# State space scan: which engine sums the four turning products, where they are kept, and how the cosine's argument is made

## The reference, cut to what matters

```
a_re, a_im = mag * cos(ang), mag * sin(ang)
bu = einsum('blgc,gpc->blgp', u, bb)            # complex input to each state
s[t] = a * s[t-1] + bu[t]                       # complex, over the 512 tokens
y = einsum('blgp,gcp->blgc', s_re, c_re) - einsum('blgp,gcp->blgc', s_im, c_im) + d * u
```

```
s_re = z0*cos - z1*sin
s_im = z0*sin + z1*cos
y    = C0 . s_re + C2 . s_im                     # C0, C2: scaled output matrices, summed over states
```

## Time and profile before

| | us |
|---|---|
| median of 3 runs (lowest to highest) | 3302.62 (3302.15 to 3303.47) |
| the profiled execution, whole / its span | 3305.22 / 3303.4 |
| PE busy | 2876.7 (87%) |
| DVE busy | 1712.5 (52%) |
| ACT busy | 1058.2 (32%) |
| POOL busy | 173.4 (5%) |

### The profile page before, as it was taken

How to read it: one execution, slowest core, us unless ns; L and a number is a source line. 1 busy time by engine, 2 the same in 40 slices (tenths; PEclk the granted TensorE clock), 3 DMA queues, 4 the chain that set the end, 5 groups by cost and what they waited for, 6 DMA issues and landing times.

```text
span 3303.4 us, 35265 instructions
## 1 busy us (share of the span) xinstructions
PE 2876.7 (87%) x13044; PEld 2335.9 (71%) x13044; DVE 1712.5 (52%) x2707; ACT 1058.2 (32%) x1557; POOL 173.4 (5%) x152
## 2 busy tenths in 40 slices
PE   2989996999999798889879998777667798999999
PEld 1865585999999477767658886545444577888887
DVE  8657776554645444334254443333688743444443
ACT  3334424221221423222342223343333232232222
POOL 0000000000000000000000000000666000000000
PEclk7989998999999878877989999876788897999999
DMA  5300051322323001000112222110111121222222
GB/s 202 111 32 1 1 171 53 128 96 99 126 98 122 24 13 39 32 20 26 59 56 95 95 95 83 51 39 26 45 48 48 48 87 45 96 95 95 94 90 95
DMA packets 68002, 237.97 MB, mean 72 GB/s; under 512 B 7680, under 2 KB 8192, under 8 KB 67776
## 3 DMA queue, kind: packets, MB, share of 16 engines
q1 hardware_dynamic: 64224, 229.23, 20.6%
q10 hardware_dynamic: 3680, 7.42, 0.7%
HBM read 234.52 MB, written 2.10 MB: 72 GB/s over the span
## 4 chain that ended last, share of the span: by engine, by line
PE 75%; DVE 17%; ACT 4%; issue 3%; DMA 0%; POOL 0%; ACTq 0%; DVEq 0%; SPq 0%
PE DP L416 20%; PE DP L418 19%; PE DP L417 19%; PE XP L787 2%; PE XP L1065 2%; DVE PR L2175 2%; PE XP L909 2%; DVE TQ L2171 2%; PE XP L529 1%; DVE MPROD L476 1%; DVE TQ L556 1%; DVE PR L2165 1%; DVE HL L545 1%; PE DP L929 1%; PE XP L999 1%
## 5 line engine op out<-in xcount | busy, mean ns | idle before, releaser
L416 PE MATMUL DP<-HH,WL 128*128 128x512 f32 (+1 forms) x1920 | 743.2, 387 | 118.0 <-DVE WL L409 72.2
L417 PE MATMUL DP<-HH,WH 128*128 128x512 f32 (+1 forms) x1920 | 716.4, 373 | 0.0
L418 PE MATMUL DP<-HL,WH 128*128 128x512 f32 (+1 forms) x1920 | 715.3, 373 | 0.0
L409 DVE TENSOR_TENSOR WL<-RAW,WH 128x1024 fp32r<-128x1024 f32 x327 | 400.5, 1225 | 338.8 <-ACT WH L400 328.7
L416 PEld LDWEIGHTS DP<-HH,WL 128*128 128x128 f32 x1920 | 371.3, 193 | 193.2 <-DVE WL L409 82.8
L416 PE MATMUL DP<-A,WL 128*128 128x384 f32 (+1 forms) x1296 | 476.5, 368 | 21.7 <-DVE A L2202 11.1
L400 ACT ACTIVATE WH<-RAW 128x1024 fp32r<-128x1024 f32 x327 | 343.7, 1052 | 467.2 <-PE DP L418 413.1
L418 PE MATMUL DP<-A,WH 128*128 128x384 f32 (+1 forms) x1296 | 471.7, 364 | 0.0
L417 PE MATMUL DP<-A,WH 128*128 128x384 f32 (+1 forms) x1296 | 471.6, 364 | 0.0
L417 PEld LDWEIGHTS DP<-HH,WH 128*128 128x128 f32 x1920 | 369.8, 193 | 57.4 <-issue 13.3
L418 PEld LDWEIGHTS DP<-HL,WH 128*128 128x128 f32 x1920 | 368.5, 192 | 47.3
(11 more groups left out here) (322 smaller groups left out, 3544.3 us busy)
## 6 DMA issues: line engine op xcount, KB each, us to landing
RAW<-in_stream SPq DMA_DIRECT2D x423, 512.0 KB, 3.3
MATS<-in_ssm ACTq DMA_DIRECT2D x16, 256.0 KB, 2.6
X<-in_x SPq DMA_DIRECT2D x8, 384.0 KB, 9.8
BW<-in_rel ACTq DMA_DIRECT2D x4, 512.0 KB, 3.6
out<-X SPq DMA_DIRECT2D x8, 256.0 KB, 2.4
COND<-in_cond SPq DMA_DIRECT2D x1, 1024.0 KB, 5.0
CONST<-in_const SPq DMA_DIRECT2D x1, 256.0 KB, 5.0
COS<-in_rope SPq DMA_DIRECT2D x1, 256.0 KB, 11.6
```

The source lines that it names most:

```text
L409: dve.tensor_tensor(WL[:, w, :], RAW[:, nxt.u % RING, :], WH[:, w, :].bitcast(F32), ALU.subtract).then_inc(raw_done[nxt.u % RING], 1)
L416: pe.matmul(out, al, bh, start=first, stop=False)
L417: pe.matmul(out, ah, bh, start=False, stop=False)
L418: return pe.matmul(out, ah, bl, start=False, stop=last)
```

## The change

Four things are done together.

- **The sums.** VectorE's two sums of products (L2178) go. TensorE multiplies all four products and adds them up in PSUM: CM(0) with the first, CM(3) with the second, CM(2) with the third and the fourth. CM(3), which was scratch, now holds minus CM(0), made by a new GpSimd instruction.
- **The tile.** The four products go to a tile of their own, PAIRS, in place of PR. It lies at the address of HH, whose columns for the context tokens aren't used in this stage.
- **The waits.** The wait for `ssm_out` on VectorE moves from ahead of the first products (L2165 before) to ahead of the last products. TensorE waits for each product by itself.
- **The cosine.** cos(x) is taken as sin(quarter turn - |x|). ScalarE makes the magnitude (`Abs`) from TURN into TR, and GpSimd's L685 and L687 go.

```diff
+        with ExitStack() as s7:
+            PAIRS = sb(s7, "PAIRS", [P, KT, T])
...
+        def TURNED(k):
+            return PAIRS[:, 2 * k:2 * k + 2, LAT:T]
...
             def turns(i):
                 pool.tensor_tensor(TURN[:, :], TURN[:, :], TR[:, 0:LAT], ALU.subtract).then_inc(sem("ssm_turns"), 1)
-                pool.wait_ge(sem("ssm_turns"), 2 * i + 1)
-                pool.tensor_scalar(TR[:, 0:LAT], TURN[:, :], 0.25, None, ALU.is_gt).then_inc(sem("turn_back"), 1)
-                pool.wait_ge(sem("turn_back"), i + 1)
-                pool.tensor_tensor(TR[:, 0:LAT], TURN[:, :], TR[:, 0:LAT], ALU.subtract).then_inc(sem("ssm_turns"), 1)
...
             def outputs_scaled(i):
                 pool.tensor_tensor(CM(2), CM(1), CM(2), ALU.subtract).then_inc(sem("ssm_c"), 1)
+                pool.wait_ge(sem("ssm_c"), 3 * i + 1)
+                pool.tensor_scalar(CM(3), CM(0), -1.0, None, ALU.mult).then_inc(sem("ssm_c"), 1)
...
             def ssm_outputs(i):
-                pe.wait_ge(sem("ssm_c"), 2 * i + 2)
+                pe.wait_ge(sem("ssm_c"), 3 * i + 3)
...
-                for q, k in enumerate((0, 2)):
-                    pe.wait_ge(sem("ssm_state"), 2 * i + q + 1)
-                    last = pe.matmul(XP[:, 2 + t % 2, :], CM(k), PR[:, k, :], start=(j == 0 and q == 0), stop=(j == 3 and q == 1))
+                for k, c in enumerate((0, 3, 2, 2)):
+                    pe.wait_ge(sem("ssm_products"), 4 * i + k + 1)
+                    last = pe.matmul(XP[:, 2 + t % 2, :].rearrange("p (a n) -> p a n", a=2), CM(c), TURNED(k),
+                                     start=(j == 0 and k == 0), stop=(j == 3 and k == 3))
...
             def trig(i):
-                act.wait_ge(sem("ssm_turns"), 2 * i + 1)
+                act.wait_ge(sem("ssm_turns"), i + 1)
+                act.activation(TR[:, 0:LAT], TURN[:, :], ACT.Abs).then_inc(sem("turn_back"), 1)
                 act.activation(TRIG[:, i % 2, 0, :], TURN[:, :], ACT.Sin, scale=TWO_PI).then_inc(sem("ssm_trig"), 1)
-                act.wait_ge(sem("ssm_turns"), 2 * i + 2)
-                act.activation(TRIG[:, i % 2, 1, :], TR[:, 0:LAT], ACT.Sin, scale=TWO_PI, bias=QUARTER[:, 0:1]
+                act.wait_ge(sem("turn_back"), i + 1)
+                act.activation(TRIG[:, i % 2, 1, :], TR[:, 0:LAT], ACT.Sin, scale=-TWO_PI, bias=QUARTER[:, 0:1]
                                ).then_inc(sem("ssm_trig"), 1)
...
             def turned(i):
                 if i:
                     dve.wait_ge(sem("ssm_products"), 4 * i)
-                    dve.wait_ge(sem("ssm_out"), i)
...
                 dve.wait_ge(sem("ssm_z"), 2 * i + 2)
+                if i:
+                    dve.wait_ge(sem("ssm_out"), i)
                 for k, (z, q) in enumerate([(0, cos), (1, sin), (0, sin), (1, cos)]):
-                    dve.tensor_tensor(PR[:, k, :], TQ[:, z, 0:LAT], q, ALU.mult).then_inc(sem("ssm_products"), 1)
-                dve.wait_ge(sem("ssm_products"), 4 * i + 4)
-                for z, op in ((0, ALU.subtract), (2, ALU.add)):
-                    dve.tensor_tensor(PR[:, z, :], PR[:, z, :], PR[:, z + 1, :], op).then_inc(sem("ssm_state"), 1)
+                    dve.tensor_tensor(TURNED(k), TQ[:, z, 0:LAT].rearrange("p (a n) -> p a n", a=2),
+                                      q.rearrange("p (a n) -> p a n", a=2), ALU.mult).then_inc(sem("ssm_products"), 1)
```

More of the change, by code:

```diff
@@ L1541, in _ @@
                     if i >= 1:
-                        act.wait_ge(sem("ssm_c"), 2 * i)
+                        act.wait_ge(sem("ssm_c"), 3 * i)
                         act.wait_ge(sem("ssm_driven"), i)
```

## The result

| | before | after |
|---|---|---|
| median of 4 runs (lowest to highest), us | 3303.05 (3302.15 to 3306.21) | 3231.26 (3229.80 to 3231.63) |
| ratio, 95% interval | | 0.9777 (0.9765 to 0.9790) |
| span of the profiled execution, us | 3303.4 | 3229.6 |
| first L2165 (L2171) to the end of the stage, us | 255.3 | 184.0 |
| mean of its first 14 periods, us | 16.3 | 11.6 |

The forecast was 3235 us with the range 3220 to 3256. Of the 73.8 us by which the span is shorter, 71.3 lie inside the stage and 1.8 at its start; the 707 us behind it differ by 0.7.

What follows compares the result with a forecast made beforehand. The stage was bound by a serial sum over VectorE and TensorE, 16.40 us a period. 14 x 11.8 + 2.0 + 1.0 + 10.7 + 10.8 = 189.7 us against 255.3; with the start 67.5 less: 3235 us, range 3220 to 3256.

Steps and rivals of the forecast that it cites:

- first L2165 earlier: Start of the stage: without L685 and L687, less 1.1 us for Abs and the sine, the first products start 1.85 us earlier.
- period without L2153: One iteration of the changed loop, start to start of the first products: 11.8 us, taken between 11.65 and 12.0.
- L2153 three times, and TensorE late once: Additions to the 14 periods: 2.0 us for L2153 on VectorE in three iterations, about 1 us for TensorE once.
- fifteenth iteration: The iteration ahead of the last, with no angle work left: 10.7 us, set by TensorE.
- tail: Last iteration: first product done 7.2 us after L2165, then four matmuls with their end 3.6 us, 10.8 us in all.
- The removed wait and sums: VectorE goes from its last product to L409 and the next L2165 without waiting for outputs; both L2178, 1.3 us, go.
- GpSimd: Its 7.2 us of work per iteration ends 9.1 us after the last product, beside the scans (3.4), leaving last products at 2.54.
- ScalarE and its queue: Abs and the later sine table load: next angle out at 4.0 us, ahead of GpSimd's 5.2 at the earliest; nothing charged.
- The four matmuls: TensorE's output matmuls: 0.86 us each at full clock, 3.44 together, ending some 1.7 us after the last product.
- The clock: TensorE's granted clock in the changed loop: 1.00, with one pause of some 1 us per 11.8.
- The slower rival: TensorE at half clock for the whole loop, 20.7 us a period: 3371 us; chance 0.03.
- Rival 1: GpSimd slides back beside VectorE's last products too, period 12.95, products at 3.8: 3251 us; chance 0.11.

Runs made afterwards that it cites:

- The extra instructions: Changed kernel plus one GpSimd instruction per iteration that nobody waits for: a two-tensor subtraction in one run (3230.44 us), a one-tensor multiplication in another (3226.63 us).
- one added wait: Changed kernel, same instructions, with GpSimd's subtraction L690 waiting for VectorE's first product from PSUM of the next iteration: 3219.47 us.
- taking the work away: Changed kernel with the angle's whole turns taken off by ScalarE and one VectorE instruction in place of GpSimd: 3221.70 us.
- the added multiplication: Changed kernel plus one GpSimd multiplication of one 128x512 SBUF tensor by a constant per iteration, which nobody waits for: 3226.63 us.
- The extra subtraction: Changed kernel plus one GpSimd subtraction of two 128x512 SBUF tensors per iteration, which nobody waits for: 3230.44 us.

## Why the prediction was right, point by point

The steps against the trace, in us:

| step of the prediction | forecast | measured |
|---|---|---|
| first L2165 earlier | 1.85 | 1.84 |
| period without L2153 | 11.8 | 11.50 |
| L2153 three times, and TensorE late once | 3.0 | 1.4 (162.4 for 14 periods, less 14 x 11.5) |
| fifteenth iteration | 10.7 | 10.21 |
| tail | 10.8 | 11.39 |
| stage | 189.7 | 184.0 |

- **The removed wait and sums.** Right: the chain stays on VectorE. By the runs with one part undone, the moved wait is worth 12.5 us, the sums 21.0 and the cosine 12.6. Together that is 46 of 72 us: with two parts in place the loss of the third is partly covered. The periods say the same: 16.3 before, 12.1 to 12.8 with one part undone, 11.5 with all. The tile of its own wasn't undone by itself; without it the moved wait isn't allowed, as L2171 would write over what L1070 reads.
- **GpSimd.** The size was right and the place wrong. I had VectorE's scans at 3.4 and its last products free at 2.5. The scans took 2.71 and the products 3.56. The stretch in all was 0.12 + 0.36 + 1.05 = 1.5 us against the 1.45 that the rows gave. That these agree is in part luck. One subtraction costs about as much wherever it meets two SBUF inputs (1.04 us on the scans before, 1.05 on the products now), but my reason for free products was wrong: I had GpSimd's work at 7.2 us, and it took 8.4 (L698 at 2420.26 to L690's end at 2428.64), the new scaling L704 0.96 of it where I had 0.5. It ran into the products, which began 7.9 us after the last product of the iteration before, and not 9.1.
- **The error of the period** is 11.8 - 11.5 = 0.3 us, 14 times, 4 us of the 5.7 by which the stage's sum was too long. Half of it is the 0.15 that I put on top of 11.65 for a share by time. The extra instructions that cost nothing or less show that there is no share that goes by GpSimd's busy time alone. The other half is in the plain list, L416 above all, which is 1.13 us from start to start and not 1.24.
- **ScalarE and its queue.** Right. The table load stands behind the wait for the products, and the next angle is out 4.0 us after the last product, as forecast, ahead of GpSimd.
- **The four matmuls.** Right in price: six records in 2.84 us, a record being 0.59 long, lie (2.84 - 0.59) / 5 = 0.45 apart, and TensorE kept its clock. The tail came out 0.6 us longer, half of it because the last iteration's scans still took 2.70: the scaling of the output matrices alone stretches them, and in the earlier trace rows it was over before they began.
- **The clock.** Right: 1.00, the upper level, in the middle of the stage, with TensorE idle for 5.9 of 100 us. The Trainium skill, TensorE: Matmul & The Clock Gate, section "A second HAM failure mode", warns that small pauses between groups can make it swing; pauses like the 0.39 and 0.48 us ahead of L1070 did not make it do so.
- **The slower rival** needed TensorE at half clock all the time, and nothing of it was seen. Rival 1 (the sharing stays whole) was half right in its picture, and the sign that I had named for it, products at 3.8, did come in every iteration that had the subtraction on the fourth product; it was wrong in its sum, as the scans were freed. So that sign didn't tell the rival from the forecast. I had named the scans at 3.4 and the products at 2.5 as signs of being right, and neither was seen.

## What to carry to other kernels

Read a period as a list of one engine and ask what it waits for between its own instructions; a wait for another engine, once a tile of its own removes it, also hides that engine's work and keeps TensorE's clock. Where GpSimd runs beside VectorE, look at which of VectorE's instructions read two SBUF tensors and which read PSUM, and put GpSimd's own two-input instructions beside the latter, by a semaphore if need be: one added wait here was worth as much as taking the work away. And test a price by adding the work as well as by removing it: the added multiplication made the periods shorter and so showed that what had looked like a price was a place.

## What the runs showed of the hardware that was not expected

- A GpSimd instruction with two SBUF inputs and a VectorE instruction with two SBUF inputs hold each other up for most of their length. In the changed kernel the first two products take 2.36 us together when L690 (1.52 us) starts 0.3 us ahead of the second of them, 1.07 more than two alone. Beside VectorE's products from PSUM the same subtraction took 1.30 us and they took 2.47; in all 13 profiles each of the 64 products from PSUM took 0.67 to 0.69 us, whatever GpSimd did. The Trainium skill, SBUF — State Buffer, section "Who interferes with whom", says that a VectorE instruction with two SBUF inputs contends with a GpSimd instruction that reads SBUF, and one with at most one such input (outside its two-port modes) doesn't; the trace agrees.
- With one input on GpSimd it costs less for each instruction: beside L704 and L687 (0.96 and 2.62 us, one input each) the two scans took 2.71 us in place of 2.35, and no product beside such an instruction took more than 1.10 us in place of 0.68. It adds up all the same: with the extra multiplication the four last products took 3.34 us, without the large subtraction beside them. Why the two scans took 3.39 us in the earlier trace rows follows from L683, the subtraction, which met the second of them: that scan took 2.24 us, and 1.20 alone.
- Both sides pay. L702, the same form as L701 with its 0.46 us, took 0.91 beside VectorE's sums. The extra subtraction that started 0.3 us behind a weight split took 2.02 us and the split its usual 1.21; when it started 0.3 us ahead, it took 1.47 and the split 2.28.
- The pattern can lock in. In the changed kernel GpSimd starts when the outputs are done, and VectorE's list decides when that is. With the wait back, the old cosine or the extra multiplication, nearly every iteration repeats the same collision. In the changed kernel itself the subtraction falls by turns on the second, the fourth and the first product; in the run with the extra subtraction the pattern changed once, at the first L2153, from periods of 10.95 to 11.61. What picks a regime in a given kernel was not tested.
